# A hybrid decoder layer on one NeuronCore: transpositions of the attention moved two items on, the output projection in two passes, and its first inputs loaded from the Pool's queue

## The reference, cut to what matters

```python
u = rmsnorm(h, attn_norm_g) @ w_in
y_rwkv = rwkv7_mix(u[..., :RWKV_COLS], ...)          # recurrence, group norm, + bonus, * gate
y_fox = fox_mix(u[..., RWKV_COLS:], ...)
    # per head, per block of 128 queries i:
    #   scores = q_i @ k[:i+1].T * scale + bias ; probs = softmax(scores) ; out_i = probs @ v[:i+1]
h = h + concat([y_rwkv, y_fox]) @ w_out              # the output projection: 2048 x 2048
hn = rmsnorm(h, ffn_norm_g)
h = h + (silu(hn @ w_gate) * (hn @ w_up)) @ w_down
h = h + sigmoid(rmsnorm(h, ...) @ ple_gate_w + ple_gate_b) * rmsnorm(p @ ple_proj, ...)
```

## Time and profile before

| | us |
|---|---|
| three runs | 2842.83, 2845.57, 2849.9 |
| their median | 2845.57 |
| the profiled execution, device time | 2851.47 |
| its span, first to last instruction | 2849.8 |
| PE busy | 2745.6 (96%) |
| DVE, ACT, POOL busy | 1139.2, 1007.6, 215.9 |
| tail and output projection (first product of the tail's finish to first product of the FFN) | 966.18 to 1198.0 |

### The profile page before, as it was taken

The page is one execution under the profiler, slowest core; times in us unless marked ns, Lnnn a source line. Parts: engine busy times, 40 slices in busy tenths (PEclk is TensorE's granted clock), DMA queues, the critical chain, the costliest instruction groups (busy, mean ns, idle before and its releaser), DMA issues.

```text
span 2849.8 us, 41116 instructions
## 1 busy us (share of the span) xinstructions
PE 2745.6 (96%) x15562; PEld 2173.3 (76%) x15562; DVE 1139.2 (40%) x1669; ACT 1007.6 (35%) x1427; POOL 215.9 (8%) x344
## 2 busy tenths in 40 slices
PE   7999999999999889999999999999999999999998
PEld 5776666666667558888888888888888888888787
DVE  6642652553454333333333333333333333334544
ACT  5434533543443443343322333223332222234421
POOL 2000110110120011100000000000000000001300
PEclk9999999999999989999999999999999999999999
DMA  4221221222212232232233222232222322223232
GB/s 162 76 81 56 67 83 39 78 68 61 64 59 75 89 109 98 96 103 96 91 91 105 96 96 97 87 108 98 96 94 86 105 98 96 96 87 105 96 121 78
DMA packets 107733, 255.34 MB, mean 90 GB/s; under 512 B 35144, under 2 KB 37704, under 8 KB 107624
## 3 DMA queue, kind: packets, MB, share of 16 engines
q1 hardware_dynamic: 106352, 249.73, 27.3%
q0 software_dynamic: 1280, 4.20, 0.4%
HBM read 244.90 MB, written 8.98 MB: 89 GB/s over the span
## 4 chain that ended last, share of the span: by engine, by line
issue 75%; PE 15%; POOL 3%; DVE 3%; ACT 2%; DMA 1%; SPq 1%; POOLq 0%; DVEq 0%; ACTq 0%
PE bank L291 4%; PE bank L288 4%; PE bank L292 4%; PE bank L325 2%; POOL probs L988 1%; POOL scratch_pool L116 1%; DMA x_raw<-xT 1%; DVE acc_x L1548 0%; DVE w_lo L283 0%; POOL sg_t L980 0%; ACT w_hi L276 0%; POOL acc_e L1763 0%; POOL carried L1015 0%; PE bank L447 0%; POOL M_t L1002 0%
## 5 line engine op out<-in xcount | busy, mean ns | idle before, releaser
L283 DVE TENSOR_TENSOR w_lo<-raw,w_hi 128x1024 fp32r<-128x1024 f32 (+1 forms) x476 | 542.0, 1141 | 973.9 <-ACT w_hi L276 963.9
L276 ACT ACTIVATE w_hi<-raw 128x1024 fp32r<-128x1024 f32 (+1 forms) x476 | 468.6, 987 | 1039.8 <-PE bank L292 994.6
L288 PE MATMUL bank<-hn_hi,w_hi 128*128 128x512 f32 x1664 | 648.1, 389 | 0.0
L292 PE MATMUL bank<-hn_hi,w_lo 128*128 128x512 f32 x1664 | 647.3, 389 | 0.0
L291 PE MATMUL bank<-hn_lo,w_hi 128*128 128x512 f32 x1664 | 647.3, 389 | 0.0
L288 PE MATMUL bank<-in_hi,w_hi 128*128 128x512 f32 x1086 | 472.4, 435 | 52.3 <-DVE in_lo L1536 11.6
L291 PE MATMUL bank<-in_lo,w_hi 128*128 128x512 f32 x1086 | 444.9, 410 | 0.0
L292 PE MATMUL bank<-in_hi,w_lo 128*128 128x512 f32 x1086 | 431.6, 397 | 0.0
L288 PEld LDWEIGHTS bank<-hn_hi,w_hi 128*128 128x128 f32 x1664 | 312.3, 188 | 65.6 <-issue 0.5
L292 PEld LDWEIGHTS bank<-hn_hi,w_lo 128*128 128x128 f32 x1664 | 312.3, 188 | 64.9
L291 PEld LDWEIGHTS bank<-hn_lo,w_hi 128*128 128x128 f32 x1664 | 312.3, 188 | 64.9 <-issue 0.5
(11 more groups left out here) (237 smaller groups left out, 2118.6 us busy)
## 6 DMA issues: line engine op xcount, KB each, us to landing
raw<-w_gu SPq DMA_DIRECT2D x176, 512.0 KB, 3.4
raw<-w_mix SPq DMA_DIRECT2D x136, 512.0 KB, 3.6
raw<-w_down SPq DMA_DIRECT2D x64, 384.0 KB, 3.1
raw<-w_down SPq DMA_DIRECT2D x64, 320.0 KB, 2.8
raw<-ple_gate SPq DMA_DIRECT2D x32, 512.0 KB, 3.5
x_raw<-xT SPq DMA_DIRECT2D x4, 1024.0 KB, 12.0
h_t<-xT SPq DMA_DIRECT2D x4, 1024.0 KB, 8.8
out<-h_t POOLq DMA_DIRECT2D x16, 256.0 KB, 2.3
```

The source lines that it names most:

```text
L276: nc.scalar.activation(w_hi[:, ring_slots(par2, half), 0:cols[half]], raw[:, half, 0:cols[half]], ACT.Copy).then_inc(hi_ready, 1)
L283: nc.vector.tensor_tensor(w_lo[:, s, 0:cols[half]], raw[:, half, 0:cols[half]], w_hi[:, s, 0:cols[half]].bitcast(F32), ALU.subtract).then_ ...
L288: nc.tensor.matmul(out, w_h, x_hi, start=start, stop=False, skip_group_check=True)
L292: return nc.tensor.matmul(out, w_l, x_hi, start=False, stop=stop, skip_group_check=True)
```

## The change

1. `PARTS`: the transpositions of an item stand 10 slots behind its scores (before: 7) and its product with the values 12 (before: 9). As items come every 5 slots, the transpositions of item q now stand directly behind the scores of item q+2. This holds for all four groups.
2. The output projection is done in two passes. The rows of `w_out` are reordered on the host so that the 12 tiles from memory are input tiles 0 to 11 and the four late ones (two of the recurrence, two of the attention of group 3) are 12 to 15. The early pass multiplies 12 tiles for each of the 16 output tiles and adds the sum to `h_t`; the late pass multiplies the other four and adds again. In the tail, each of the 96 slots now holds one tile (three matmuls): slots 0 to 23 the first two slabs in turns, slots 24 to 95 six more slabs of 12 tiles; the other eight early slabs follow in a loop. In the late pass a slab of weights holds four output tiles of four input tiles each.
3. The 12 tiles are loaded by the Pool's queue, each group of three as soon as the last slab of the input projection has used these tiles of `in_lo` (semaphore `x_used`), instead of by SP after its end. `h_t` is loaded in the tail, a quarter before each of the first four early slabs; the SBUF layout is rearranged so that `h_t` lies over buffers no longer used then, and the finish keeps its intermediate values in `AR` instead of `t1` and `t2`.

In the rows below from the built programs, lines of the change are numbered otherwise: 299, 302, 303 are the three products, 460 and 463 the scores, 476 the transpositions, 1687 the addition to `h_t`, 1104 `hn_lo`, 294 `w_lo`.

The diff, cut to what the prediction speaks of:

```diff
-PARTS = {"scores": 0, "exp": 1, "scale": 2, "turn": 7, "values": 9}
+TAIL_TILES = [*range(6), *range(8, 14), 6, 7, 14, 15]
+PARTS = {"scores": 0, "exp": 1, "scale": 2, "turn": 10, "values": 12}
...
+EARLY, LATE = 12, KT - 12
+EARLY_COLS = (EARLY // 2 * P,) * 2
+LATE_SLABS = LATE * OUT_SLABS // KT
+TAIL_SLABS = 6
+TAIL_SLOTS = EARLY * (2 + TAIL_SLABS)
...
+    AHEAD = 3
+    cut_at = {2 * (i - AHEAD) + 2: i for i in range(AHEAD, EARLY)} | {26: 12, 28: 13, 54: 14, TAIL_SLOTS - 1: 15}
...
@@ SP
-            sp.wait_ge(weights_used, 2 * N_OUT)
-            sp.wait_ge(S("y_rwkv_stored"), 32 * (GROUPS - 1))
-            sp.wait_ge(S("o_stored"), 32 * (GROUPS - 1) + 1)
-            for i in range(4):
-                kt = TAIL_TILES[3 * i]
-                sp.dma_start(in_lo[:, kt:kt + 3, :].bitcast(F32), y_dram[kt:kt + 3].rearrange("k p t -> p k t")
-                             ).then_inc(S(f"y_landed_{i}"), 16)
-            load_slab(sp, N_OUT + 2, d["w_mix"][N_OUT + 2])
-            sp.wait_ge(S("in_ready"), 2 * KT)
+            sp.wait_ge(tile_evacuated, N_OUT)
+            sp.wait_ge(S("fox_qk_ready"), 4 * GROUPS)
+            sp.wait_ge(S("fox_v_turned"), 2 * GROUPS)
+            sp.wait_ge(S("Y_ready"), NC * GROUPS)
             for i in range(4):
                 sp.dma_start(h_t[:, 4 * i:4 * i + 4, :], x_quarter(i)).then_inc(S(f"input_landed_{i}"), 16)
+                load_slab(sp, N_OUT + 2 + i, d["w_mix"][N_OUT + 2 + i], EARLY_COLS)
...
@@ PE
+            for i in range(EARLY):
+                for j in range(2):
+                    tail(2 * i + j)
...
+                    pe.wait_ge(S("in_ready"), KT + i + 1)
+                    last = three_products(psum[j][:], ring_slots(j, i // HALF), i % HALF * P, in_hi[:, i, :],
+                                          in_lo[:, i, :], i == 0, i == EARLY - 1)
...
+            for m in range(TAIL_SLABS):
+                def side(kt):
+                    tail(EARLY * (2 + m) + kt)
+                multiply_slab(pe, N_OUT + 2 + m, m % 2, in_hi, in_lo, kts=(EARLY // 2, EARLY // 2), side=side)
+            with pe.Fori((2 + TAIL_SLABS) // 2, OUT_SLABS // 2) as i:
+                for j in range(2):
+                    multiply_slab(pe, N_OUT + 2 * i + j, j, in_hi, in_lo, kts=(EARLY // 2, EARLY // 2))
             pe.wait_ge(S("in_ready"), 2 * KT)
+            for u in range(LATE_SLABS):
+                n = N_LATE + u
+                for r in range(LATE):
+                    o = LATE * u + r
+                    if r % 2 == 0:
+                        pe.wait_ge(lo_ready, 2 * n + r // 2 + 1)
+                    if o < 2:
+                        pe.wait_ge(tile_evacuated, N_LATE - 1 + o)
+                    else:
+                        pe.wait_ge(*added_late(o - 2))
+                    for k in range(LATE):
+                        last = three_products(...)
...
@@ ACT, beside its attention and finish in each slot st of the tail
+                if st in cut_at:
+                    cut(cut_at[st])            # rounds input tile i to in_hi; DVE's cut(i) makes in_lo
...
+                if m is not None and kt in (1, 6):
+                    round_slab(act, N_OUT + 3 + m, (m + 1) % 2, EARLY_COLS, halves=(kt // 6,))
...
+            for o in range(OUT_SLABS):         # the late pass
+                u, r = divmod(o, LATE)
+                ffn_norm[0](act, o, added_late(o), o, 1)
+                if r % 2:
+                    round_slab(act, N_LATE + u + 2, u % 2, halves=(r // 2,))
...
@@ POOL, before its attention of the tail
+            for i in range(4):
+                pool.wait_ge(S("x_used"), 4 * (GROUPS - 1) + i + 1)
+                pool.dma_start(in_lo[:, 3 * i:3 * i + 3, :].bitcast(F32),
+                               y_dram[y_at(3 * i):y_at(3 * i) + 3].rearrange("k p t -> p k t")
+                               ).then_inc(S(f"y_landed_{i}"), 16)
```

More of the change, by code:

```diff
@@ L267, in load_slab @@
             after(sp, lo_ready, 2 * n + half - 1)
-            sp.dma_start(raw[:, half, 0:cols[half]], src[:, sum(cols[:half]):sum(cols[:half + 1])]
+            sp.dma_start(raw[:, half, 0:cols[half]], src[:, start + sum(cols[:half]):start + sum(cols[:half + 1])]
                          ).then_inc(raw_landed[half], 16)
@@ L307, in multiply_slab @@
                                       kt == 0, kt == sum(kts) - 1, burst)
+                if used is not None and kt % 3 == 2 and kt < EARLY:
+                    last.then_inc(used, 1)
                 kt += 1
@@ L1328, in _ @@
-            with pe.Fori(1, OUT_SLABS // 2) as i:
-                for j in range(2):
-                    multiply_slab(pe, N_OUT + 2 * i + j, j, in_hi, in_lo)
+                    last = three_products(psum[j][:], ring_slots(j, i // HALF), i % HALF * P, in_hi[:, i, :],
+                                          in_lo[:, i, :], i == 0, i == EARLY - 1)
+                    if (i, j) == (HALF - 1, 0):
+                        last.then_inc(weights_used, 1)
+                    if i == EARLY - 1:
+                        last.then_inc(weights_used, 1 + j)
@@ L1608, in out_pair, with early_pair @@
+            for i in range((2 + TAIL_SLABS) // 4, 4):
+                dve.wait_ge(S(f"input_landed_{i}"), 32)
+            add_to_residual(1 + TAIL_SLABS, N_OUT + 1 + TAIL_SLABS, 1)
+            subtract_slab(dve, N_OUT + 3 + TAIL_SLABS, 1, EARLY_COLS)
+            def early_pair(i, last):
                 for j in range(2):
                     o, n = 2 * i + j, N_OUT + 2 * i + j
-                    subtract_slab(dve, n + 2, j, halves=(0,))
+                    next_cols = gate_slab_cols if last else EARLY_COLS
+                    subtract_slab(dve, n + 2, j, next_cols, halves=(0,))
@@ new lines, in _ @@
+            with dve.Fori((2 + TAIL_SLABS) // 2, OUT_SLABS // 2 - 1) as i:
+                early_pair(i, False)
+            early_pair(OUT_SLABS // 2 - 1, True)
+            for o in range(OUT_SLABS):
+                u, r = divmod(o, LATE)
+                n = N_LATE + u
+                if r % 2:
+                    dve.wait_ge(weights_used, 2 * n + r // 2 + 1)
+                else:
+                    dve.wait_ge(late_done, 2 * u + r // 2 + 1)
+                nc.vector.tensor_tensor(h_t[:, o, :], h_t[:, o, :], psum[r % 2][:], ALU.add
+                                        ).then_inc(added_late(o)[0], 1)
+                if o > 0 and o % 2 == 0:
+                    v, half = (o - 1) // LATE, (o - 1) % LATE // 2
+                    subtract_slab(dve, N_LATE + v + 2, v % 2, halves=(half,))
+                ffn_norm[1](dve, o, o)
```

253 lines of the change are left out of this document (134 added, 119 removed).

## The result

The changed kernel takes 2807.5 us (median of 4 runs, 2801.8 to 2812.6) against 2847.7 for the kernel before on the same chip: ratio 0.986, 95% interval 0.984 to 0.988. The forecast was 2806. That is 40 us less. The two profiled executions lie further apart, 2801.76 against 2851.47, and 8 of these 50 us are not the change's, as a comparison by stretch shows.

The account below looks back on a forecast made before the run. PE, busy 96%, bounds the kernel; its waits and slow clock can be gained. 15 + 28.2 - 3 - 0 = 40 us takes the profiled 2851.47 to 2811.5, as a median 2806 us; range 2796 to 2824.

Parts of the forecast that it names:

- step a: Attention of groups 1 to 3: transpositions 10 slots behind the scores remove PE's waits for POOL's product, 15 us.
- Its two terms: Per group in attention of groups 1 to 3: 3.9 us of PE waits plus 1.4 us lost at half-speed clock.
- item 15: Attention item in groups 1 to 3 whose wait is as long as the three slots; 0.3 us a group left.
- step b: Tail: one tile in every slot removes PE's idle time and the low clock; 28.2 us, less 3 for new waits.
- the sum: Tail forecast: 19.7 us idle and 7 + 1.5 us of clock gained, 3 us of new waits taken off.
- The new waits for the cuts: Tail's start: PE waits for input tiles that ACT rounds and DVE subtracts; 3 us, bounds 0 and 8.6.
- step c: Late pass of the output projection: POOL's sum-of-squares circle of 2.1 to 2.6 us stays below PE's 2.72; cost 0.
- Group waits come back: Groups 1 to 3: DVE's row maximum and ACT's exp may be late; gain 25 us, 2821 us, chance 0.12.
- Late pass held by POOL: Late pass: POOL's sum stands still during DVE instructions with two SBUF inputs; 11.5 us, 2817 us, chance 0.12.
- Tail's start late: Tail's start: tile loads above 8.9 us, or cuts behind ACT's table changes; 2818 to 2825 us, chance 0.06.
- Nothing gained: Groups and tail: the two places only trade waits; 2843 us, chance 0.04.
- Weights too late for short slabs: Early slabs in the tail: load, rounding and subtraction of weights take 12 us against PE's 8.2; 2859 us, chance 0.06.

Follow-up runs that it names:

- kernel 2: Kernel before with only the transpositions 9 and values product 11 slots behind the scores, output projection in one pass: 2827.6 us, ratio 0.993 to 0.996.
- kernel 1: Kernel before with only the transpositions 10 and values product 12 slots behind the scores, output projection in one pass: 2830.9 us, ratio 0.994 to 0.997.
- kernel 7: Changed kernel with the input tiles rounded and subtracted five tiles ahead of their first product instead of three: 2805.1 us, ratio 0.984 to 0.988.
- kernel 8: Changed kernel with a second POOL operation of the same size before each sum of squares: 2827.8 us, ratio 0.992 to 0.996.
- kernel 9: Changed kernel with the tail's first twelve input tiles loaded by SP behind its last weights load of the slab before: 2811.6 us, ratio 0.986 to 0.990.
- kernel 10: Changed kernel with POOL's four tile loads all issued when the last old tiles are used: 2812.8 us, ratio 0.987 to 0.991.
- turn 9 and 8: Transpositions 9 or 8 slots behind the scores: with 9, 2827.6 us on the kernel before, 2803.7 on the changed kernel; with 8, 2803.4 on the changed kernel.
- kernel 3: Changed kernel with transpositions 7 and values product 9 slots behind the scores as before, so the two passes alone: 2821.9 us, ratio 0.990 to 0.993.
- kernel 4: Changed kernel with transpositions 9 and values product 11 slots behind the scores: 2803.7 us, ratio 0.984 to 0.988.
- kernel 5: Changed kernel with transpositions 8 and values product 10 slots behind the scores: 2803.4 us, ratio 0.985 to 0.989.
- kernel 12: Changed kernel with bonus product three tiles later, input tiles cut five ahead, transpositions 9 and values 11 slots behind the scores: 2797.0 us, ratio 0.982 to 0.986.

## Why the prediction was right

**Groups (step a), 15 us predicted, 13.7 measured (15.2 in kernel 2, 10.4 in kernel 1, whose clock fell in two groups).** The mechanism was right: POOL's product with too little distance, and the slow clock behind its longest wait. Its two terms were off against each other, and part of the agreement is luck. With 10 slots a wait of 2.0 us is still there, at another place; that the clock stayed up behind it in all three groups of the changed kernel's profile is chance, worth up to 3 x 1.6 = 4.8 us, as kernels 1 and 7 to 10 show. The waits were worth less than their 3.9 us, since 3.1 us of others (RWKV preparation on DVE and ACT) came up when PE ran earlier. I had left 0.3 us for waits, at item 15, where none was left. Busy time fell more than by the 1.4 us that I put down for the clock: 4.0 in groups 1 and 2. Of it the clock is 1.6 (group 3 of the kernel before, which kept it, is busy 104.41 us against 105.99). 1.2 is what the joined transpositions save, which I had denied. The rest, 1.2, is there with turn 9 and 8 too. That it goes with the four waits is my reading, no run takes it apart.

**Tail (step b), 25 us predicted, 28.0 measured, 27.0 in kernel 3.** Idle time fell from 19.7 us to 2.2 (the sum: to 3), and the granted clock is 1.00, as the sum had it. From the tail's start to the FFN PE's busy time fell from 212.0 to 201.8 us, 10.3 against the 8.5 that the sum gave for the clock; idle and busy together make the 2.8 us that the sum was short. The new waits for the cuts were 2.0 us, not 3. The loads landed in 5.3 us, inside 2.3 to 7.0. Their cover up to the slab's end, which I had put at 8.9 us, was 13.0 (931.0 to 944.1), since the recurrence stands between the tiles; up to the first cut it was 9.7. Kernels 9 and 10 show what the cover is worth: PE waits 4.3 and 4.8 us when it is gone. The rule of the Trainium skill ("Trainium Kernel Development and Optimization", Key Constraints) that queues share the engines, and another queue saves only issue time, is not contradicted: POOL's queue made the wait no shorter (4.8 against 4.3 us with SP's), though the two places differ by 2 us. The second addition to `h_t` is seen only as 0.2 us of wait.

**Late pass (step c), 0 predicted, 0 measured.** Output tiles are 2.72 us apart, with no wait. POOL's sum took 1.29 to 1.51 us, against 1.275 to 1.767 in the rows.

**The rivals.** *Group waits come back*: 3.1 of 3.9 us did, at other places than named; the group is 0.5 us longer than with 9 slots, and the gain of the groups stayed. *Late pass held by POOL*: not here, though kernel 8 shows that the circle does bind once it is longer than 2.72. Its worst case, POOL standing still in every DVE instruction with two inputs, would be stretches of 0.75 to 2 us; the sum is stretched by 0.2 us in the changed kernel and by 0.5 in kernel 8 (1.28 and 1.79). What was wrong in it is the number of instructions that count: in the rows above POOL stands still for what is left of the one under way when it begins, and in the late pass that was 0.09 or 0.35 us of `hn_lo`. The rule of the Trainium skill ("GPSIMD Engine Reference", Specifications) that DVE instructions with two SBUF inputs contend with GpSimd for the interfaces agrees with these rows. *Tail's start late*: no; kernels 9 and 10 are that rival made true for the loads. *Nothing gained*: no. *Weights too late for short slabs*: PE did not wait for weights in the 204 us.

That 2807.5 lies 1.5 us from the forecast is partly luck: the runs of the changed kernel lie 11 us apart with the granted clock, and the misses in (a) and (b) have opposite signs.

## What to carry to other kernels

Where one engine's in-order list waits for a short chain on others, look first for the longest wait and give the list that much distance: here one slot of at least 0.68 us gave 12.9 us and the second 2.3 more, and the third took 1.5 us back, because another wait was next. Where a stage ends in a chain with little beside it, distance alone moves the wait (1.3 to 2.4 us gained in the old tail), and only more independent work in every slot fills it (27 us). And compare two profiles by stretches that hold the same code before crediting a change with their whole difference: here 50 us of difference held 8 that were not the change's.

## What the runs showed of the hardware

- Behind the same idle time PE's granted clock does or does not fall. Behind the 2.0 us wait at line 373 (360 in kernel 1) it stayed at 1.00 in the changed kernel's three groups, and in kernels 1, 7 and 9 it fell in two of three. Of all the profiled groups whose longest wait was 1.9 to 2.1 us it fell in 17 of 30 (a part's mean clock 0.98 in place of 1.00); of those with 1.4 us or less (kernels 2, 4, 5, 12) in none of 12. A fall cost 1.6 us.
- A one-element operation on POOL took 0.19 us with DVE idle (line 116 at 991.74 in the kernel before), as on ACT, but 1.19 us where it began inside a DVE instruction with two inputs in SBUF, and it ended 0.05 us behind that instruction (line 123 at 1132.27 in kernel 8).
- POOL's sum of two tiles took 1.28 us with no such instruction before it and 1.79 with 0.66 us of such an instruction left before it. It holds the other way too: `hn_lo`, which began at 1128.13 in kernel 8 while POOL's product ran, took 1.02 us in place of DVE's 0.75.
- POOL's product of a tile with itself took 1.04 us and its sum of two tiles 1.26 at the least, with 128x512 f32 elements in both (kernel 8).
